# Router, row turns and ranks of a token tile inside the residual products of the next, six expert homes, three row buffers

## What is computed

```python
x = x + merged @ w_o
h = rmsnorm(x, norm_g)
glog = h @ w_router_group + b_router_group          # 4 groups
elog = h @ w_router_expert + b_router_expert        # 32 experts
gsel = argmax(glog); p_group = softmax(glog)[gsel]
top_v, top_i = top_k(elog[group gsel], 2)
top_w = softmax(top_v) * p_group
for e in range(32):                                 # w1, w3: 1024x256, w2: 256x1024
    he = silu(h @ w1[e]) * (h @ w3[e])
    y = y + combine[:, e:e+1] * (he @ w2[e])
out = rmsnorm(x + y, norm_final_g)
```

## Time and profile before

| | |
|---|---|
| median of three runs | 1523.73 us |
| the profiled execution, its span | 1521.15 us, 1519.5 us |
| TensorE busy | 1350.7 us (89%) |
| VectorE, ScalarE, Pool busy | 784.1, 492.6, 229.1 us |
| residual products | 1130 to 1210 us |
| experts, first up product to last down product | 1233 to 1483 us |
| mean granted clock of TensorE | 0.958 |

### The profile page before, as it was taken

The page is one execution under the profiler, slowest core; times in us unless marked ns, Lnnn a source line. Parts: engine busy times, 40 slices in busy tenths (PEclk is TensorE's granted clock), DMA queues, the critical chain, the costliest instruction groups (busy, mean ns, idle before and its releaser), DMA issues.

```text
span 1519.5 us, 19482 instructions
## 1 busy us (share of the span) xinstructions
PE 1350.7 (89%) x7202; PEld 903.1 (59%) x7202; DVE 784.1 (52%) x1707; ACT 492.6 (32%) x1155; POOL 229.1 (15%) x334
## 2 busy tenths in 40 slices
PE   7989789999999999987788899999999969878880
PEld 5545466666676766765565677777765545444440
DVE  3158877878878878878655621101113533211105
ACT  2143124665654655534655420000002211111112
POOL 3000000220320321222530000000000023222210
PEclk9999999999999999999999999999999979988995
DMA  8412332435444435344019425203215199999975
GB/s 262 121 30 54 85 111 94 135 105 161 135 127 130 145 97 139 107 147 111 17 26 193 156 94 159 56 0 116 106 53 241 65 356 414 415 416 415 414 293 215
DMA packets 148176, 247.45 MB, mean 163 GB/s; under 512 B 39540, under 2 KB 106852, under 8 KB 139156
## 3 DMA queue, kind: packets, MB, share of 16 engines
q1 hardware_dynamic: 137012, 215.10, 42.1%
q0 software_dynamic: 11072, 31.12, 6.0%
HBM read 216.50 MB, written 36.88 MB: 167 GB/s over the span
## 4 chain that ended last, share of the span: by engine, by line
PE 47%; DVE 7%; ACT 3%; issue 3%; DMA 2%; POOL 1%; SPq 0%; DVEq 0%; POOLq 0%; ACTq 0%
PE psum L1413 14%; PE psum L1680 9%; PE psum L662 9%; PE psum L1580 5%; PE psum L1696 4%; PE psum L1417 3%; DVE arena L2277 1%; ACT arena L1993 1%; PE psum L1398 1%; ACT arena L1915 1%; PE psum L1317 1%; DVE arena L2716 1%; PE psum L1362 1%; POOL arena L1116 1%; DMA wring<-in_w_in 1%
## 5 line engine op out<-in xcount | busy, mean ns | idle before, releaser
L662 PE MATMUL psum<-hT,wring 128*128 128x320 f32 x1024 | 296.9, 442 | 29.2 <-DVE arena L627 17.4
L662 PEld LDWEIGHTS psum<-hT,wring 128*128 128x128 f32 x1024 | 195.9, 194 | 116.4 <-DVE arena L627 18.9
L662 PE MATMUL psum<-wring 128*128 128x320 f32 x768 | 218.2, 434 | 0.0
L662 PEld LDWEIGHTS psum<-wring 128*128 128x128 f32 x768 | 146.4, 191 | 61.9 <-issue 1.0
L1417 PE MATMUL psum<-ident,arena 128*128 128x128 f32 (+3 forms) x950 | 139.6, 284 | 41.0 <-ACT arena L1915 11.5
L1417 PEld LDWEIGHTS psum<-ident,arena 128*128 128x128 f32 (+3 forms) x950 | 105.2, 143 | 94.8 <-issue 61.9
L1413 PE MATMUL psum<-arena,wring 128*128 128x320 f32 x512 | 138.1, 431 | 0.0
L1413 PEld LDWEIGHTS psum<-arena,wring 128*128 128x128 f32 x512 | 96.6, 189 | 41.2
L638 ACT ACTIVATE wring<-psum 128x320 f32<-128x320 f32 (+2 forms) x140 | 49.6, 379 | 188.7 <-PE psum L662 178.0
L1680 PE MATMUL psum<-wring,arena 128*64 128x256 f32 x608 | 84.3, 439 | 23.8 <-issue 21.0
L1915 ACT ACTIVATE arena<-psum 128x512 f32<-128x512 f32 (+8 forms) x155 | 71.7, 517 | 83.9 <-PE psum L1417 57.1
(11 more groups left out here) (344 smaller groups left out, 1940.9 us busy)
## 6 DMA issues: line engine op xcount, KB each, us to landing
wring<-in_w SPq DMA_DIRECT2D x38, 1024.0 KB, 21.6
arena<-in_w SPq DMA_DIRECT2D x32, 1024.0 KB, 24.7
wring<-in_w_in SPq DMA_DIRECT2D x25, 1024.0 KB, 5.5
oT<-in_w SPq DMA_DIRECT2D x14, 1024.0 KB, 21.8
hT<-in_w SPq DMA_DIRECT2D x12, 1024.0 KB, 20.5
arena<-a_rows SPq DMA_DIRECT2D x20, 512.0 KB, 4.0
arena<-in_state_ssm SPq DMA_DIRECT2D x16, 512.0 KB, 7.3
out<-arena POOLq DMA_DIRECT2D x16, 512.0 KB, 3.8
```

The costliest lines, as they stand in the source:

```text
L662: ins = nc.tensor.matmul(o[:, 0:TH], wt[:, k, :], rows[:, k, :], start=n in (1, 5, 2) and k == 0, stop=k == 3, skip_group_check=True)
```

## The change

The half products take helpers between their eight matmuls: the second turns of the tile before at k = 3 of the first half and its ranks (of the tile before that) at k = 6; the router of the tile before at k = 2 of the second half and the first turns of this tile at k = 5. VectorE's order follows. Behind the last product stand only the placement of tile 2, the ranks and placement of tile 3, and the last tile's second turns, router, ranks and placement. `XS` becomes 6 and `RS` 3. The sixth home of w1 and w3 is the memory of the residual products' operand. w2 of experts 0, 1, 2 and 5 is loaded with the weights of experts 0 to 2 ahead of the products; w2 is loaded in two DMAs. `hgT`, `ysl` and the gain's row move to other memory. The diff, cut:

```diff
-XS = 5
-RS = 4
+XS = 6
+RS = 3
...
-        rows_in, hgT, ysl = a5.take(RS, HD2), a5.take(2, KD, SLOTS), a5.take(RS, HD2)
+        h2T, xn, w2_more = a5.take(2, KD, P), a5.take(3, D), a5.take(4 * D)
+        hgT = xn[:, 2, :].rearrange("p (u k q) -> p u k q", u=2, k=KD)
...
+        rows_in, ysl_last = a5.take(RS, HD2), a5.take(HD2)
+        ysl = [arena[:, 4 * D:4 * D + HD2], arena[:, 4 * D + HD2:5 * D], ysl_last]
...
+        w2s.append([hTf[:, 2 * KD * FF:KD * T], oTf[:, 2 * KD * FF:KD * T]])
...
             def load2(e):
-                sp.dma_start(w2s[e % XS], w2[e].rearrange("(k p) n -> p k n", p=P)).then_inc(w2_loaded[e % XS], 16)
+                for k in range(2):
+                    sp.dma_start(w2s[e % XS][k], w2[e, k * P:(k + 1) * P, :]).then_inc(w2_loaded[e % XS], 16)
...
-            load13(0)
-            load2(0)
-            load13(1)
-            load13(2)
-            wait_read(sp, ("x1", NT - 1, 1))
-            load2(1)
-            load13(3)
-            load2(2)
-            load13(4)
+            for e in range(3):
+                load13(e)
+                load2(e)
+            load2(5)
+            wait_full(sp, ("x1", NT - 1, 1))
+            for e in range(3, XS):
+                load13(e)
             wait_full(sp, ("rt", NT - 1))
...
-            def x1_half(t, n):
+            def x1_half(t, n, between):
                 o = claim(pe, ("x1", t, n))
                 for k in range(KD):
+                    if k in between:
+                        between[k]()
...
+            for tt in range(NT):
+                first, second = {}, {5: lambda: rows_turned(tt, 0)}
+                if tt > 0:
+                    first[3] = lambda: rows_turned(tt - 1, 1)
+                    second[2] = lambda: router(tt - 1)
+                if tt > 1:
+                    first[6] = lambda: ranked(tt - 2)
+                x1_half(tt, 0, first)
+                x1_half(tt, 1, second)
+                if tt > 1:
                     placed(tt - 2)
             ranked(NT - 2)
+            rows_turned(NT - 1, 1)
+            router(NT - 1)
+            placed(NT - 2)
             ranked(NT - 1)
-            placed(NT - 2)
             placed(NT - 1)
...
                 ts_(var, var, 1.0 / D, EPS, ALU.mult, ALU.add).then_inc(S["row_var"], 1)
-                if 0 < t < NT - 1:
+                if t == NT - 1:
                     place_dve(dve, t - 1, link)
...
             for tt in range(NT + 1):
...
+                if tt > 0:
                     turned_rows(tt - 1, 1)
                     scale(tt - 1)
                 if tt < NT:
-                    residual(tt, 1)
-                    turned_rows(tt, 0)
...
+                    residual(tt, 0)
+                if 1 < tt < NT:
+                    place_dve(dve, tt - 2, link)
                 if tt > 0:
                     select_dve(dve, tt - 1, link)
-            place_dve(dve, NT - 2, link)
+                if tt < NT:
+                    turned_rows(tt, 0)
+                    residual(tt, 1)
             place_dve(dve, NT - 1, link)
```

More of the change, by code:

```diff
@@ L202, in plan_banks @@
     for tt in range(NT + 1):
-        if tt < NT:
-            b.add(("x1", tt, 0), six)
-        if 0 < tt < NT:
+        if tt == NT:
+            b.add(("rank", tt - 2), six)
             b.add(("h2", tt - 1, 1), six)
-        if 1 < tt < NT:
-            b.add(("rank", tt - 2), six)
[L209 to L213, removed]
+            b.add(("rt", tt - 1), six)
+            b.add(("rank", tt - 1), six)
+            continue
+        b.add(("x1", tt, 0), six)
+        if tt > 0:
+            b.add(("h2", tt - 1, 1), six)
+        if tt > 1:
+            b.add(("rank", tt - 2), six)
+        b.add(("x1", tt, 1), six)
         if tt > 0:
             b.add(("rt", tt - 1), six)
+        b.add(("h2", tt, 0), six)
         if tt == 2:
             b.add(("slots",), (7,))
-    b.add(("rank", NT - 2), six)
-    b.add(("rank", NT - 1), six)
     b.add(("tot",), (6,))
@@ L477, in hybrid_layer @@
         w2_first, x1 = a5.take(2 * D), a5.take(NT, D)
-        h2T, xn = a5.take(2, KD, P), a5.take(3, D)
-        rows_in, hgT, ysl = a5.take(RS, HD2), a5.take(2, KD, SLOTS), a5.take(RS, HD2)
+        h2T, xn, w2_more = a5.take(2, KD, P), a5.take(3, D), a5.take(4 * D)
+        hgT = xn[:, 2, :].rearrange("p (u k q) -> p u k q", u=2, k=KD)
         hsil, hetm, heT = a5.take(2, HF), a5.take(2, HF), a5.take(2, 2, SLOTS)
@@ L492, in hybrid_layer @@
         at_pos, at_blk = a5.take(2, 2, 2, SLOTS), a5.take(2, 2, NE)
+        rows_in, ysl_last = a5.take(RS, HD2), a5.take(HD2)
+        ysl = [arena[:, 4 * D:4 * D + HD2], arena[:, 4 * D + HD2:5 * D], ysl_last]
         wringf = wring.rearrange("p s k n -> p s (k n)")
         w13 = [v.rearrange("p (c k f) -> p c k f", c=2, k=KD) for v in
-               (wringf[:, 1], oTf[:, 0:2 * KD * FF], wringf[:, 2], wringf[:, 0], hTf[:, 0:2 * KD * FF])]
-        w2s = [v.rearrange("p (k n) -> p k n", k=2) for v in
-               (w2_first, arena[:, 0:2 * D], arena[:, 2 * D:4 * D], xn.rearrange("p t d -> p (t d)")[:, 0:2 * D],
+               (wringf[:, 1], oTf[:, 0:2 * KD * FF], wringf[:, 2], wringf[:, 0], hTf[:, 0:2 * KD * FF], arena[:, 0:2 * KD * FF])]
+        w2s = [[v[:, 0:D], v[:, D:2 * D]] for v in
+               (w2_first, w2_more[:, 0:2 * D], w2_more[:, 2 * D:4 * D], xn.rearrange("p t d -> p (t d)")[:, 0:2 * D],
                 h2T.rearrange("p u k q -> p (u k q)"))]
+        w2s.append([hTf[:, 2 * KD * FF:KD * T], oTf[:, 2 * KD * FF:KD * T]])
         squares_out = oTf.rearrange("p (t d) -> p t d", t=NT)
         nothing = ssq[:, 5, 7:8]
-        fin_row = arena[:, 4 * D:5 * D]
+        fin_row = kvtm[:].rearrange("p t w -> p (t w)")[:, 0:D]
         ypart = wring.rearrange("p s k n -> p (s k n)")[:, 0:2 * NT * D].rearrange("p (t c d) -> p t c d", t=NT, c=2)
@@ L968, in _ @@
             for i in range(RS):
-                sp.wait_ge(scattered[i], 16 * NE // RS)
+                sp.wait_ge(scattered[i], 16 * len(range(i, NE, RS)))
             final_sp(sp, 0)
@@ L1143, in _ @@
                                         bass.IndirectOffsetOnAxis(ap=slot_row[:, e:e + 1], axis=0),
-                                        ysl[:, e % RS, :], None, bounds_check=4 * T - 1, oob_is_err=False) \
+                                        ysl[e % RS], None, bounds_check=4 * T - 1, oob_is_err=False) \
                     .then_inc(scattered[e % RS], 16)
             for i in range(RS):
-                pool.wait_ge(scattered[i], 16 * NE // RS)
+                pool.wait_ge(scattered[i], 16 * len(range(i, NE, RS)))
         def ssd_pe(pe, g, turn):
@@ L1635, in spill_placed @@
                     filled(ins, ("spill",))
[L1637 to L1648, removed]
-                if tt > 0:
-                    router(tt - 1)
-                if 1 < tt < NT:
+            for tt in range(NT):
+                first, second = {}, {5: lambda: rows_turned(tt, 0)}
+                if tt > 0:
+                    first[3] = lambda: rows_turned(tt - 1, 1)
[4 more added lines that the diff above has]
+                x1_half(tt, 1, second)
+                if tt > 1:
                     placed(tt - 2)
             ranked(NT - 2)
+            rows_turned(NT - 1, 1)
+            router(NT - 1)
+            placed(NT - 2)
             ranked(NT - 1)
-            placed(NT - 2)
             placed(NT - 1)
@@ L1690, in down @@
                 pe.wait_ge(S["heT_ready"], e + 1)
-                pe.wait_ge(w2_loaded[e % XS], 16 * (e // XS + 1))
+                pe.wait_ge(w2_loaded[e % XS], 32 * (e // XS + 1))
                 if e >= 2:
@@ L1696, in down @@
                         ins = mm(pbank(4 + e % 2)[m * SLOTS:(m + 1) * SLOTS, :], heT[:, e % 2, k, :],
-                                 w2s[e % XS][:, k, HD2 * m:HD2 * (m + 1)], start=k == 0, stop=k == 1)
+                                 w2s[e % XS][k][:, HD2 * m:HD2 * (m + 1)], start=k == 0, stop=k == 1)
                 ins.then_inc(S["dn_full"], 1)
@@ L2075, in _ @@
                         act.wait_ge(scattered[e % RS], 16 * (e // RS))
-                    fn(ysl[:, e % RS, :], pbank(4 + e % 2), ACT.Copy).then_inc(S["dn_read"], 1)
+                    fn(ysl[e % RS], pbank(4 + e % 2), ACT.Copy).then_inc(S["dn_read"], 1)
                 if e == 16:
@@ L2694, in _ @@
             for tt in range(NT + 1):
-                if tt < NT:
-                    residual(tt, 0)
-                if 0 < tt < NT:
+                if tt > 0:
                     turned_rows(tt - 1, 1)
@@ L2700, in _ @@
                 if tt < NT:
-                    residual(tt, 1)
-                    turned_rows(tt, 0)
-                if tt == NT - 1:
-                    turned_rows(tt, 1)
-                    scale(tt)
+                    residual(tt, 0)
+                if 1 < tt < NT:
+                    place_dve(dve, tt - 2, link)
                 if tt > 0:
                     select_dve(dve, tt - 1, link)
-            place_dve(dve, NT - 2, link)
```

(11 more changed lines are left out.)

## The result

The changed kernel takes 1577.05 us (median of four runs, 1570.22 to 1578.4), the kernel before 1524.84 beside it: ratio 1.034, 95% interval 1.032 to 1.036, or 52 us slower. The forecast was slower with 1547, range 1523 to 1566. The sign and the mechanism were right, the size was less than half of what came (23 us forecast, 52 measured). The profiled execution of the changed kernel has a span of 1576.4 us, 56.9 above the 1519.5 of before.

A forecast was written before the change was run, and what follows sets the result against it. The prediction took late gathers, not the weight stream, as the new bound: r(0) 1246.9 plus 13 pairs of 18.0 us, the last experts to 1507.1, tail 35.7, span 1542.8; with run overhead 1547.0 us, range 1523 to 1566.

The forecast's parts named there:

- the length of a pair: Expert loop: two successive experts take 18.0 us, bounds 16.35 and 19.2, against 12.04 at full clock without the stall.
- The landing: Expert loop: a gather's rows arrive 7.2 us after issue, the median of 32, whatever the depth of the weight backlog.
- the clock loss: Expert loop: TensorE's slower clock behind each stall costs 1.6 us a pair, bounds nothing and 2.8.
- the split of w2: Weight loads: w2 in two DMAs adds 32 issues on SP, costed at nothing, at most 0.4 us once.
- Part 1: Interleaved residual products: no late waits, last add starts at 1212.1, first gather at 1228.2, first output read 1.0 us later.
- Part 2: Early loads and sixth home: 26 experts instead of 27 left to stream, 7.6 us less, 6.6 after the later start.
- Part 3: Three row buffers in the expert loop: gathers wait one iteration longer, stalling every second expert by about 4.5 us.
- the formula of the prediction: Expert loop: 9.45 us from output read to turns, 6.9 to the next read, plus clock loss; time 1313.0 + 13 p.
- (a): Expert loop: gathers land in time, the weight stream stays the bound and the saved transfer is banked, 1517 us; chance 0.12.
- (b): Expert loop: the stall comes but the clock holds, 1525.5 us, up to 1533 for half the loss; chance 0.15.
- (c): Expert loop: two slow pieces a pair or landings of 8 us, pairs of 19.5 to 21, 1566 to 1586 us; chance 0.10.
- (d): First gather: the store gates it, so reordering does not advance it; a quick store lowers all by 3.3 us; no chance given.

The follow-up runs named there:

- a_again: The changed kernel as it is, run again for a comparison on one chip: 1575.97 us, ratio 1.034 to the kernel before.
- a_early: The changed kernel, three row buffers, each gather issued one place earlier on Pool's queue, ahead of the scatter: 1518.1 us, ratio 0.996.
- a_four: The changed kernel with a fourth row buffer for the gathers alone, outputs still in three: 1518.5 us, ratio 0.996.
- a_five: a_early with five homes instead of six, without the early load of w2 of expert 5: 1523.99 us, ratio 1.000.
- a_best2: a_early with expert 3's w1 and w3 loaded earlier and expert 5's held until the last tile's store has landed: 1516.45 us, ratio 0.994.
- a_light: The changed kernel without the w3 loads of experts 6 to 31, a third less weight, outputs not the reference's: 1536.9 us.
- b_three: The kernel before with three row buffers instead of four and nothing else of the change: 1564.5 us.

## Why the prediction was right, and where it was wrong

The sign and the path were right: the gather that comes too late in front of every second expert. What failed is the length of a pair in the sum. The landing was put at 7.2 us and measured 8.6, the clock loss at 1.6 us and measured 2.9, and the split of w2, which lengthens both, was put at nothing. Together they turned the forecast 18.0 us a pair into 20.5, thirteen times over.

**Part 1 held.** Last residual add 1212.1 forecast, 1212.40 measured; first gather 1228.2 forecast, 1228.13 measured, with the store as what is late, and no waits of TensorE inside the products. That the second agrees to 0.1 us is luck: in a_again, the same kernel, the residual products began 3.0 us later (1133.43 against 1130.42) and the first gather went out at 1231.78. The first output read came 0.8 us later than forecast (1247.66): the first gather landed in 4.6 us instead of 4.2, and the first up product took 5.06 us instead of 4.71.

**Part 2 held in the runs that let it show.** 6.6 us was the gain if the stream stays the bound; a_early and a_four gained 6.4 and 6.0, and a_five lost it all again. The wrong line in that part is the one on the split of w2: "I cost them at nothing". I looked only at SP's queue, on which the second issue adds 0.4 us (0.81 against 0.38), and not at the gathers, which landed 0.5 us later with it. It is 10.8 of the 52 us, and it comes through the landing and the clock below, not beside them.

**Part 3 held in its mechanism.** Thirteen stalls, in front of the turns of every second expert, the output read of the other expert following 6 us behind, the stream below its rate, gathers 30 and 31 no longer gating: from output read 26 to 31 it took 26.3 us, as summed. Two terms of the pair were too small:

- *The landing*: 7.2 us taken; the gathers of experts 4, 6, 8 to 26 landed in 8.1 to 9.3 us in the changed kernel, 8.6 on average, 1.4 more. The median of 32 in the earlier trace rows is taken mostly in the saturated stretch. The single 7.8 in the same group comes from a loop not yet held up by the stream, and by that it was the nearer row. It was issued 3.2 us behind a load of w2 (1244.86), but that alone does not make a landing long: in the changed kernel the gathers between the gating ones (experts 5, 7 to 25) are also issued 3.1 us behind a load of w2 and landed in 7.5 us on average. What sets the gating ones apart, from expert 6 on, is that SP had issued no load for some 13 us before these loads; whether that is the cause no run shows.
- *The clock*: 1.6 us a pair taken. From the turns at 1258.74 to the end of the output read at 1268.74 it is 10.0 us, and 6.9 without clock loss, so 3.1; all thirteen pairs lose 2.3 to 3.1, 2.9 on average. Of the two rows the one behind the longer gap had shown 2.8. I reasoned that part of the slow piece would fall into the longer stall; it did not. The up products behind the stalls take 5.4 to 6.2 us, and the turns in front of them, which the sum had at full clock because in the kernel before no stall stood in front of them, add nearly 0.5 us more. In a_again, behind stalls of much the same length (4.4 to 6.2 us), the loss is 1.5 to 2.9, 2.5 on average; so the exact size differs from one execution to the next.

With 7.8 and 2.8 from the same rows the way from output read to turns is 10.05 us, and the formula of the prediction gives p = 10.05 + 6.9 + 2.8 = 19.8 and 1570 us, still 7 short; with the measured 20.5 it gives 1579.5, and 1577 was measured. The slope of 13 us for each microsecond of a pair was the right warning: both disputed terms were multiplied by it, and the range should have carried both at their upper bound together. One sign came out differently as well: with the slow piece in each pair the up products stood 12.2 and 8.5 us apart (1259.79, 1268.31, 1280.49), where 12 and 6 were forecast.

**The rivals.** (a), that the gathers land in time, did not come; a_early and a_four, at 1518.1 and 1518.5, show that its 1517 was the right price of it. (b) fell with every up product behind a stall; its "up to 1533 for half of the loss" should read 1536. (c), 1566 to 1586, is what happened, at the 10 per cent I gave it: landings above 8 us and more clock lost, though in one longer slow piece a pair and not in two. (d), the quick store, is a_best2. The rule that the prediction takes from the Trainium skill's page "DMA: Bandwidth & Descriptors", section "Queues, rings and completion order", that an engine goes round its queue rows, agrees with what was asked of it: landings of gathers did not grow where those of the weights took 25 us. It says nothing of the 7.2 against 8.6, and a_light shows that the amount of weight in flight still counts a little.

## What to carry to other kernels

A buffer count is only half of a prefetch distance; the other half is where the refill stands on its engine's queue. Here three buffers cost 40 us and more with the gather behind a scatter, and nothing with it moved one place ahead, so before a buffer is taken away write down for one iteration what the refill is queued behind, when it is issued and when its rows are wanted. Where a term is multiplied by the iterations, take it from the row whose surroundings are those of the new schedule and not from the median, and count a stall of TensorE twice, once as idle time and once as the slower clock behind it.

## What the runs showed of the hardware that I had not expected

- A stall of 4 to 6 us costs TensorE 1.5 to 3.1 us more afterwards (after, a_again, b_three); 4 us of matmuls without use in front of a late DMA gave 37 us back (1577 to 1539) over twelve stalls, some 32 of them by the clock.
- A gather of one expert's rows landed in 7.2 us (median) where the queue is always full (share 1.02). At a share of 0.87 the gathers that TensorE waited for, the first behind a pause in the loads, took 8.6 us and the ones between them 7.5. Less traffic on average did not mean a faster landing; the cause is open.
- Loading a matrix of 1 MB as two DMAs of 512 KB instead of one cost 10.8 us (ratios 1.034 and 1.027) in a kernel that waits for its gathers; the mechanism is open.
